# Sixteen instead of twelve adaptation tiles summed by GpSimd, each loaded in two halves

## The reference

```python
def ada_chunks(cvec, w, b):
    m = jax.nn.silu(cvec) @ w + b
    return jnp.split(m[..., None, :], 6, axis=-1)
...
for layer in range(DEPTH):
    sh_m, sc_m, gt_m, sh_f, sc_f, gt_f = ada_chunks(c, w_ada[layer], b_ada[layer])
    csh_m, ... = ada_chunks(c_ctx, w_ada[layer], b_ada[layer])
```

## Time and profile before

| | before |
|---|---|
| three runs, median | 1927.93 us |
| the profiled execution's own time | 1923.98 us |
| its span | 1922.2 us |
| PE busy | 1884.9 us (98%) |
| DVE busy | 1281.9 us (67%) |
| ACT busy | 916.0 us (48%) |
| POOL busy | 247.9 us (13%) |
| loads of w_ada by POOL | 12 of 1 MB |

### The profile page before, as it was taken

How to read it: one execution, slowest core, us unless ns; L and a number is a source line. 1 busy time by engine, 2 the same in 40 slices (tenths; PEclk the granted TensorE clock), 3 DMA queues, 4 the chain that set the end, 5 groups by cost and what they waited for, 6 DMA issues and landing times.

```text
span 1922.2 us, 28534 instructions
## 1 busy us (share of the span) xinstructions
PE 1884.9 (98%) x11790; PEld 1621.2 (84%) x11790; DVE 1281.9 (67%) x1666; ACT 916.0 (48%) x1288; POOL 247.9 (13%) x175
## 2 busy tenths in 40 slices
PE   9999999999999999999999999999999999979998
PEld 7888969887888888888889878988888889679997
DVE  6776796776677669777664564755554367857774
ACT  5334565334533555633464265533333255855554
POOL 0000007732757600000000110000000000000000
PEclk9999999999999999999999999999999999989999
DMA  8675436776577643776452221323223223025552
GB/s 312 254 272 210 176 135 244 278 264 222 204 270 271 229 162 108 269 281 245 154 187 88 110 78 67 110 88 121 88 88 110 91 85 132 12 88 176 176 197 88
DMA packets 50960, 323.78 MB, mean 168 GB/s; under 512 B 5472, under 2 KB 9744, under 8 KB 12816
## 3 DMA queue, kind: packets, MB, share of 16 engines
q1 hardware_dynamic: 39024, 270.09, 38.9%
q10 hardware_dynamic: 10080, 39.28, 5.4%
q0 software_dynamic: 1728, 12.58, 1.7%
HBM read 320.86 MB, written 1.07 MB: 167 GB/s over the span
## 4 chain that ended last, share of the span: by engine, by line
PE 78%; DVE 14%; ACT 4%; issue 2%; DMA 0%; ACTq 0%; DVEq 0%; SPq 0%
PE ps L558 76%; DVE s_wl L1948 5%; DVE s_tmp L2047 3%; ACT s_wh L1275 2%; DVE s_xx L1948 2%; DVE s_big L2247 1%; PE ps L917 1%; DVE s_tmp L2065 1%; PE ps L774 0%; PE ps L751 0%; DMA s_raw<-in_ffn_gate 0%; ACT s_big L1447 0%; DVE s_big L2070 0%; DVE s_tmp L2469 0%; DVE s_X L2445 0%
## 5 line engine op out<-in xcount | busy, mean ns | idle before, releaser
L558 PE MATMUL ps<-s_xx,s_wh 128*128 128x512 f32 (+1 forms) x3328 | 894.0, 347 | 1.4 <-DVE s_wl L2018 0.6
L1948 DVE TENSOR_TENSOR s_wl<-s_raw,s_wh 128x2048 fp32r<-128x2048 f32 x213 | 493.6, 2319 | 287.7 <-ACT s_wh L1275 287.7
L558 PE MATMUL ps<-s_xx,s_wl 128*128 128x256 f32 (+1 forms) x2208 | 668.6, 303 | 0.4 <-DVE s_xx L2472 0.4
L558 PEld LDWEIGHTS ps<-s_xx,s_wh 128*128 128x128 f32 x3328 | 579.9, 190 | 88.6 <-issue 5.7
L1275 ACT ACTIVATE s_wh<-s_raw 128x2048 fp32r<-128x2048 f32 x213 | 403.7, 1906 | 112.8 <-PE ps L558 108.0
L558 PEld LDWEIGHTS ps<-s_xx,s_wl 128*128 128x128 f32 x2208 | 419.0, 190 | 18.8 <-issue 2.7
L558 PE MATMUL ps<-s_wh,s_hl 128*128 128x512 f32 (+1 forms) x608 | 232.6, 383 | 2.9 <-DVE s_tmp L2047 2.4
L558 PE MATMUL ps<-s_wh,s_hh 128*128 128x512 f32 (+1 forms) x608 | 230.3, 379 | 0.0
L558 PE MATMUL ps<-s_wl,s_hh 128*128 128x512 f32 (+1 forms) x608 | 230.3, 379 | 0.0
L558 PE MATMUL ps<-s_wh,s_xx 128*128 128x256 f32 x928 | 179.2, 287 | 0.0
L1391 ACT ACTIVATE s_tmp<-s_tmp 128x512 f32<-128x512 f32 x44 | 27.8, 632 | 299.8 <-DVE s_tmp L2065 299.8
(11 more groups left out here) (239 smaller groups left out, 1852.3 us busy)
## 6 DMA issues: line engine op xcount, KB each, us to landing
s_raw<-in_ffn_down SPq DMA_DIRECT2D x44, 1024.0 KB, 4.7
s_raw<-in_w_up SPq DMA_DIRECT2D x44, 1024.0 KB, 4.7
s_raw<-in_ffn_gate SPq DMA_DIRECT2D x43, 1024.0 KB, 4.8
s_raw<-in_ffn_up SPq DMA_DIRECT2D x43, 1024.0 KB, 4.8
s_big<-in_w_ada ACTq DMA_DIRECT2D x34, 1024.0 KB, 5.9
s_raw<-in_w_down SPq DMA_DIRECT2D x22, 1024.0 KB, 4.7
s_raw<-in_w_in SPq DMA_DIRECT2D x18, 1024.0 KB, 4.9
s_X<-in_w_ada POOLq DMA_DIRECT2D x12, 1024.0 KB, 7.2
```

What stands on the lines that cost most here:

```text
L558: return pe.matmul(o, lhsT, rhs, start=start, stop=stop, skip_group_check=True)
L1948: dve.tensor_tensor(wide(wl, u), raw[:, u % SLOTS, :].rearrange("p (k n) -> p k n", k=8), f32(wide(wh, u)), SUB).then_inc(*w_low.tick(u))
```

## The change

Tiles 32 to 35 go from PE's `fill` to POOL's `sum_rows`, which now does sixteen. The four fills after j = 1 and j = 3 of (`ffn2`, 1) disappear (and with them four loads issued by ACT). The places of `row_sums` on PE move: before, tiles 36 to 39 at down n = 2 of (`ffn2`, 0), 40 to 43 after j = 4 and 44 to 47 at down n = 7 of (`ffn1`, 1); now 32 to 35 after j = 4 and 36 to 39 at down n = 2 of (`ffn2`, 0), 40 to 43 after j = 1 and 44 to 47 after j = 10 of (`ffn1`, 1). POOL loads each tile in two halves with a semaphore each: the first half of the next tile is issued when the first half of this one is folded, the second when the tile is done. A half is folded as four multiplies, one add of 128 x 512 and adds of 128 x 256.

```diff
 ADA_AT = {("ffn1", 0): {2: 1, 4: 2, 6: 2, 8: 2}, ("ffn2", 0): {1: 2, 4: 2, 7: 2}, ("ffn1", 1): {1: 1, 4: 2, 7: 2},
-          ("ffn2", 1): {1: 2, 3: 2, 5: 2, 7: 2}}
+          ("ffn2", 1): {5: 2, 7: 2}}
 SUMS_AT = {("ffn1", 0): {},
-           ("ffn2", 0): {13: 36},
-           ("ffn1", 1): {4: 40, 18: 44}, ("ffn2", 1): {}}
+           ("ffn2", 0): {4: 32, 13: 36},
+           ("ffn1", 1): {1: 40, 10: 44}, ("ffn2", 1): {}}
...
-            def load_rows(f):
-                pool.dma_start(rows, a["w_ada"][f].rearrange("p (k n) -> p k n", k=8)).then_inc(*rows_in.tick(f))
+            def load_half(f, h):
+                pool.dma_start(rows[:, 4 * h:4 * h + 4, :], a["w_ada"][f][:, 1024 * h:1024 * h + 1024].rearrange(
+                    "p (k n) -> p k n", k=4)).then_inc(*rows_in[h].tick(f))
+
+            def fold_half(f, h):
+
+                pool.wait_ge(*rows_in[h][f])
+                for k in range(4 * h, 4 * h + 4):
+                    pool.tensor_scalar(rows[:, k, :], rows[:, k, :], strip_c[:, k, 0:1], None, MUL).then_inc(
+                        *multiplied.tick((f, k)))
+                pool.wait_ge(*multiplied[f, 4 * h + 3])
+                pair_ = rows[:, 4 * h:4 * h + 2, :]
+                pool.tensor_tensor(pair_, pair_, rows[:, 4 * h + 2:4 * h + 4, :], ADD).then_inc(*folded.tick((f, h)))
+                pool.wait_ge(*folded[f, h])
 
             def sum_rows(fs):
 
                 pool.wait_ge(*gated["c"])
-                load_rows(fs[0])
+                load_half(fs[0], 0)
+                load_half(fs[0], 1)
                 for f in fs:
...
+                    fold_half(f, 0)
+                    if f >= 36:
                         pool.wait_ge(*product["row sums", f // 4 * 4 - 1])
-                    pool.tensor_tensor(row_sum(f), rows[:, 0, :], rows[:, 1, :], ADD).then_inc(*rows_summed.tick(f))
+                    pool.tensor_tensor(row_sum(f), rows[:, 0, :], rows[:, 1, :], ADD).then_inc(*folded.tick((f, "first")))
+                    pool.wait_ge(*folded[f, "first"])
                     if f < fs[-1]:
-                        pool.wait_ge(*rows_summed[f])
-                        load_rows(f + 1)
+                        load_half(f + 1, 0)
+                    fold_half(f, 1)
+                    pool.tensor_tensor(row_sum(f), row_sum(f), rows[:, 4, :], ADD).then_inc(*folded.tick((f, "second")))
+                    pool.wait_ge(*folded[f, "second"])
+                    pool.tensor_tensor(row_sum(f), row_sum(f), rows[:, 5, :], ADD).then_inc(*rows_summed.tick(f))
+                    pool.wait_ge(*rows_summed[f])
+                    if f < fs[-1]:
+                        load_half(f + 1, 1)
...
-                    sum_rows(range(36, 48))
+                    sum_rows(range(32, 48))
```

More of the change, by code:

```diff
@@ L169, in program @@
         biased, cleared = (signal(n) for n in ("biased", "cleared"))
-        rows_in, rows_summed = signal("rows_in", 16), signal("rows_summed")
+        rows_in = [signal(f"rows_in{i}", 16) for i in range(2)]
+        rows_summed = signal("rows_summed")
         multiplied, folded = signal("multiplied"), signal("folded")
@@ L655, in ada_columns @@
                 pe.wait_ge(*picked[0])
-                n = 12
+                n = 8 if g == 2 else 12
                 for c in range(2):
@@ L661, in ada_columns @@
                 if g == 1:
-                    a, n = 36, 3
+                    a, n = 32, 4
                     row = const("ident").rearrange("p (i j) -> p j i", i=4)[:, 24:24 + n, :]
@@ L683, in fill @@
                     rows = slice(32 * (k % 4), 32 * (k % 4) + 32)
-                    m = mm(ps[7][rows, 256:512], c_strip(k, i), w[:, k, :], i == 0 and k < 4, i == 11 and k >= 4)
+                    m = mm(ps[7][rows, 256:512], c_strip(k, i), w[:, k, :], i == 0 and k < 4, f in (11, 23, 31) and k >= 4)
                 m.then_inc(*product.tick(("fill", f)))
@@ L691, in row_sums @@
                 for i in range(4):
-                    m = mm(ps[7][32 * i:32 * i + 32, 256:512], ones_strip((a - 36) // 4), row_sum(a + i),
+                    m = mm(ps[7][32 * i:32 * i + 32, 256:512], ones_strip((a - 32) // 4), row_sum(a + i),
                            False, False)
@@ L1294, in fill @@
                 act.wait_ge(*product["fill", f])
-                if f + 2 < 36:
+                if f + 2 < 32:
                     act.dma_start(ada_buf(f), a["w_ada"][f + 2]).then_inc(*ada_in[f % 2].tick(f + 2))
-                if f % 12 == 11:
+                if f in (11, 23, 31):
                     g = f // 12
```

## The result

The changed kernel takes 1932.83 us in the median of 10 runs (1929.92 to 1936.06), the kernel before, run beside it, 1925.01 us (1921.69 to 1930.55). The ratio is 1.0039, 95% interval 1.0027 to 1.0050: slower, by about 0.4%. The forecast was 1926 us and "the same", with 1931 us as the upper end of its own range. The profiled execution of the changed kernel took 1934.68 us, its span is 1932.9 us; before it was 1922.2, so 10.7 us have to be found in the traces.

What follows compares the result with a forecast made beforehand. PE was taken as the bound (78% of the chain), with DVE and ACT in (`ffn2`, 0). 1923.98 - 3.7 (fills) + 4.0 (DVE) + 0 (row sums) = 1924.3, or 1928.2 from the median; forecast 1926 us, own range 1921 to 1931, overall 1918 to 1938.

Steps and rivals of the forecast that it cites:

- PE's part: In (`ffn2`, 1), dropping four fills saves PE 3.7 us; moved row sums and dropped loads cost or save 0.
- POOL's tile: On POOL, a tile falls from 26.4 us to between 20.4 and 21.7, taken as 20.7, as load waits go.
- break-even: After j = 1 of (`ffn1`, 1): above 20.9 us a tile, POOL is late for the third row sums.
- The estimate by means: POOL's tile from mean instruction times: 19.9 us of work plus two issues of 0.9, 21.7 us.
- When PE comes: No row sum waits: third group ready at 533 us, PE there at 536, only 3 us in hand.
- The second group: Tiles 36 to 39 in (`ffn2`, 0): POOL ready at 451 us, PE there at 459.23 or later.
- What POOL does to DVE: In (`ffn2`, 0), busier POOL lengthens DVE's instructions on the chain: +4.0 us, between 0 and +7.3.
- The second one: POOL late to the third row sums after j = 1 of (`ffn1`, 1): 1933.9 us, or 1937.5; chance 0.16.

Runs made afterwards that it cites:

- the kernel with later places: Changed kernel, row sums taken later: tiles 36 to 39 at down n = 4, 40 to 43 after j = 4, 44 to 47 at down n = 7; 1919.06 us.
- the kernel with POOL nearly idle: The kernel with later places without POOL's 128 multiplies and 32 adds of 128x512; 1918.50 us, ratio 0.9970.
- the kernel with one wait: The kernel with later places, but tiles 36 to 39 back at down n = 2 of (`ffn2`, 0); 1925.51 us, ratio 1.0009.
- the kernel with the clock kept up: Changed kernel with 8 and 16 unused matmuls issued on PE before the waits for tiles 36 to 39 and 40 to 43; 1932.31 us, ratio 1.0037.
- the one with an add fewer: Changed kernel without POOL's add of slice 4 in each tile; 1928.53 us, ratio 1.0014.
- the one with the third group after j = 2: The kernel with later places, but tiles 40 to 43 taken after j = 2 instead of j = 4 of (`ffn1`, 1); 1924.59 us, ratio 0.9994.

## Why the prediction was wrong, point by point

The span grew by 10.7 us. By PE's timeline, in round parts: the start of (`ffn2`, 0) is 0.7 us later. From its first fill to the fill after j = 1 of (`ffn1`, 1) PE takes 199.16 us instead of 194.96, +4.2, and in these lies the first wait. From there to the last fill of the mixer it takes 265.39 instead of 255.18, +10.2, with the second wait. (`ffn2`, 1) gives back 4.15. The rest of the program differs by 0.2.

- **PE's part: right.** -3.7 was taken, -4.15 measured in the stage, in three kernels alike. DVE was no limit there.
- **POOL's tile: this step failed.** I took 20.7 us, with 20.9 as break-even; the twelve tiles to the third group took (544.06 - 284.25) / 12 = 21.65. I had chosen the lower half of my range with the argument that POOL waits for as much DVE work as before. On that argument, too, my sum was wrong: by the earlier trace rows the bare work before is 7.24 + 3 x 1.30 + 0.74 = 11.9 us a tile, not 12.4, so it grows to 12.1 and does not shrink. At equal delays the tile is 18.9 + 0.2 + 1.8 = 20.9 us, the break-even itself, and the range was 20.9 to 21.7. Measured over these twelve tiles (POOL's groups from 284 to 544.1 us), a tile has 11.5 us of multiplies, 2.7 of large adds and 5.2 of small ones, 19.4 in all, of which 7.4 are delays, against 7.0 before. So the delays grew little, but they moved: a small add that meets a low part waits for all that is left of it, whatever its own length (2.66 for 0.73 us of work), and the three of a tile lose 3.0 us where the one of before lost 0.7, while the large adds lose 0.1 instead of 1.8. The other 2.2 us are the two issues with the pause before each, 1.7, and pauses of under 0.1 us between the instructions, 0.5, which my sum had left out. The estimate by means, 21.7, was right to 0.1 us, in part by luck: its large adds were 1.1 us too dear, its small ones 0.8 too cheap, and the short pauses were missing.
- **When PE comes: the margin was smaller still.** I had PE at 536 for the third group, with 4.0 us lost in (`ffn2`, 0). Without that loss and without the first wait it would have come at 531; the kernel with later places was there at 530.9. At 21.65 us a tile, POOL is ready 13 us after that. In the changed kernel the first wait delayed PE by part of it, so the two waits show 3.7 and 7.1 us. With later places this lateness and the clock are all gone: 15.8 us.
- **The second group** was ready at 461.2 and PE there at 457.7. I had POOL at 451. Tiles of 22.86 us between 346 and 437 us, and one of 24.4 behind them, made it 10 us late. PE's place was also 1.5 us earlier than before, against the 4 us later of the forecast.
- **What POOL does to DVE: wrong, and the check was at hand.** I took +4.0, by a proportion to POOL's busy time that gave 10.2 us of delays. It cost nothing. The delays were 4.6 us, no more than before: in step with DVE's loop, POOL's adds meet the same instruction each time. And PE did not wait for them, nor is the kernel with POOL nearly idle clearly faster. The chain of waits in the earlier trace rows had gone over DVE for 129 us, and I read it as "all of this is in the chain". A chain followed back from the last event goes over DVE whenever DVE released PE last, be it by a hair. What taking a delay away there can give is bounded by PE's idle time, and that was 1.2 us in the whole stretch. What an added delay costs is only what goes beyond DVE's slack, and the chain does not show the slack. The Trainium skill, "SBUF — State Buffer", section "Who interferes with whom", says that the two exclude each other and that the one that comes second is blocked until the first is through; the half tile above agrees for adds, in both directions (2.72 instead of 2.28 us for DVE, 2.66 instead of 0.73 for POOL). I had weighed that rule for DVE alone, and left out POOL's side of it.
- **The clock: left out.** No term had the fall of the clock behind a wait. By the kernel with one wait it is 2.3 us in the span, and 2.9 at the place, on top of 3.7, and by the kernel with the clock kept up 2.7; behind the second wait three j of (`ffn1`, 1) took 35.99 us instead of 34.11, so 1.9 on top of 7.1.
- **The rivals.** The second one, POOL late to the third row sums, named the right place and direction, and its 1933.9 us lie 0.8 from the profiled execution's 1934.68. That closeness is luck: it holds 4.0 us for DVE that did not come, and it has neither the first wait nor the clock. It had 0.16. The forecast rested on 0.2 us a tile of margin, times twelve, which is less than the uncertainty of the tile time (20.4 to 21.7) that I had written down; the middle of that range, 21.05, is already past break-even, and with the bare work added up rightly its lower end is the break-even. It should have been the likeliest case.

The parts together: 0.7 at the start; 6.55 for the first wait and its clock (199.16 against 192.61 with later places); -2.35 for what the stretch gained otherwise (192.61 against 194.96; 1.2 of it is the wait for line 2047, the rest the pace of the last section and small things, with 0.44 to pay for one more group of row sums); 10.2 for the second wait (7.7 for the wait and the moved row sums, 1.9 clock, 1.2 pace, and 0.6 less in the mixer); -4.15 for the fills; -0.2 for the rest. That is 10.75.

## What to carry to other kernels

Before a delay of an engine is priced, look at how long the engine that bounds the kernel stands idle for it, and how far the delayed engine can fall back before it does; a chain of waits that goes over the delayed engine is no price. A helper that feeds a strictly ordered queue must be given a place with slack for many tiles, since a small error in its rate is multiplied by their number and everything behind the place waits; here it cost nothing to take its result later. Count a wait of TensorE with the slow clock behind it, here 2 to 3 us on top of each.

## What the runs showed of the hardware

**Two paces of PE at one granted clock.** The three j after a fill take 34.11 us in some places and 33.48 in others, with the clock at 1.00 in both: the pairs of matmuls start every 0.353 or 0.347 us. PE keeps one of the two from one fill or wait to the next. With later places, the stretch behind the second fill is the fast one (start, us):

```profile
373.26 2.37 PE L559 MATMUL ps<-s_big 128*32 128x256 f32 x40
409.04 1.93 PE L559 MATMUL ps<-s_big 128*32 128x256 f32 x32
```

and with POOL nearly idle, the same program on PE has the slow one there:

```profile
371.99 2.37 PE L559 MATMUL ps<-s_big 128*32 128x256 f32 x40
408.41 1.94 PE L559 MATMUL ps<-s_big 128*32 128x256 f32 x32
```

35.78 against 36.42 us. In (`ffn1`, 1) the kernels in which PE waited for the third group run at the slow pace from the fill after j = 4 to the end of the loop (the changed kernel, the one with dummy products, the one with an add fewer, and the one with the third group after j = 2), the other six kernels at the fast one. This is 1.2 us of the second part above, and belongs to the 5.8 us of the kernel with the third group after j = 2. What sets the pace was not found. Both paces occur with POOL nearly idle, so POOL's work is not needed for either, and the two rows of 40 matmuls above show that it is not the number of matmuls alone. Nor is it shown that the wait sets it: the six fast kernels are also those in which the row sums stand right behind the fill after j = 4 of (`ffn1`, 1), and no run separates the two.

**GpSimd in step with DVE.** I had not expected the tiles to lock onto DVE's loop, 2 x 11.43 us four times in a row, though their bare work is 12.1 us. The kernels with later places, with one wait and with dummy products do the same. The one with the third group after j = 2 does not, with the same program on POOL up to there: its tiles take 19.8 to 26.0 us in that loop. POOL had gained 1.4 us on the first tile there, and had to wait 2.0 us for PE to free the places at 376.18 us, which it does not in the others. In such a state a mean over other stretches does not give the rate, and the bare length of the work still less.
